# A trunk layer in split fp32: products of both token halves alternate, every second one from the last column to the first

## The reference

```
h = rms_norm(x, mix_pre_gain);  proj = h @ w_in            # 2048 x 10752
q, k, v, gm_uv, s5_u, gates = split(proj)
y_a = stick_breaking_attention(q, k, v) @ w_br_a           # 1024 x 2048
y_b = spatial_gating(gelu(gm_uv)) @ w_br_b                 #  512 x 2048
y_c = s5_layer(s5_u, ...) @ w_br_c                         #  512 x 2048
merged = g0 * y_a + g1 * y_b + g2 * y_c                    # g = sigmoid(gates)
x = x + rms_norm(merged @ w_out, mix_post_gain)
x = x + rms_norm(memory_cross_attention(rms_norm(x), rms_norm(mem), ...), xattn_post_gain)
gt, up = split(rms_norm(x, ffn_pre_gain) @ w_ffn_in)       # 2048 x 11264
x = x + rms_norm((silu(gt) * up) @ w_ffn_out, ffn_post_gain)  # 5632 x 2048
```

## Time and profile before

| | |
|---|---|
| time, median of 3 runs | 1493.7 us (1493.33 to 1494.33) |
| span of the profiled execution | 1491.6 us |
| TensorE busy | 1481.7 us (99%), 6712 matmuls |
| VectorE busy | 1137.2 us (76%) |
| ScalarE busy | 835.4 us (56%) |
| GpSimd busy | 151.4 us (10%) |
| HBM | 199 GB/s over the span |

### The profile page before, as it was taken

The page is one execution under the profiler, slowest core; times in us unless marked ns, Lnnn a source line. Parts: engine busy times, 40 slices in busy tenths (PEclk is TensorE's granted clock), DMA queues, the critical chain, the costliest instruction groups (busy, mean ns, idle before and its releaser), DMA issues.

```text
span 1491.6 us, 19212 instructions
## 1 busy us (share of the span) xinstructions
PE 1481.7 (99%) x6712; PEld 1220.6 (82%) x6712; DVE 1137.2 (76%) x1353; ACT 835.4 (56%) x1018; POOL 151.4 (10%) x286
## 2 busy tenths in 40 slices
PE   9999999999999999999999999999999999999997
PEld 7888887888888888888888888888888888888886
DVE  6878988855554577657576788888888888887897
ACT  6645455565666544656678455555555555555554
POOL 0000000140220000000000221012222221100000
PEclk9999999999999999999999999999999999999999
DMA  9755555565555655856463666766666667656564
GB/s 342 235 186 178 182 180 186 189 208 187 188 192 171 239 183 185 334 195 211 161 197 116 198 209 221 230 212 216 209 212 199 198 217 236 231 173 213 187 208 169
DMA packets 89859, 305.08 MB, mean 205 GB/s; under 512 B 13056, under 2 KB 13568, under 8 KB 88768
## 3 DMA queue, kind: packets, MB, share of 16 engines
q1 hardware_dynamic: 80144, 285.12, 57.6%
q0 software_dynamic: 9216, 18.63, 3.9%
q10 hardware_dynamic: 432, 0.45, 0.1%
HBM read 294.19 MB, written 2.10 MB: 199 GB/s over the span
## 4 chain that ended last, share of the span: by engine, by line
PE 99%; DMA 0%; DVE 0%; SPq 0%; ACT 0%; issue 0%; DVEq 0%
PE acc L1808 10%; PE acc L1809 10%; PE acc L1810 10%; PE acc L2128 5%; PE acc L2131 5%; PE acc L2130 5%; PE side L2130 5%; PE side L2131 5%; PE side L2128 5%; PE side L1808 4%; PE side L1809 4%; PE side L1810 4%; PE tr L1808 3%; PE tr L1809 3%; PE tr L1810 3%; PE side L2093 2%
## 5 line engine op out<-in xcount | busy, mean ns | idle before, releaser
L548 ACT ACTIVATE w_hi<-raw 128x1024 fp32r<-128x1024 f32 x299 | 315.1, 1060 | 295.4 <-PE acc L2131 90.2
L1001 DVE TENSOR_TENSOR w_lo<-raw,w_hi 128x1024 fp32r<-128x1024 f32 x262 | 320.9, 1227 | 202.0 <-ACT w_hi L529 197.7
L1006 DVE TENSOR_TENSOR w_lo<-raw,w_hi 128x1024 fp32r<-128x1024 f32 x315 | 381.5, 1222 | 102.8 <-ACT w_hi L548 92.9
L529 ACT ACTIVATE w_hi<-raw 128x1024 fp32r<-128x1024 f32 x262 | 276.9, 1059 | 281.3 <-PE acc L1810 165.6
L1808 PE MATMUL acc<-w_hi,xT_hi 128*128 128x512 f32 x504 | 198.3, 393 | 0.5 <-DVE w_lo L1001 0.5
L1810 PE MATMUL acc<-w_hi,xT_lo 128*128 128x512 f32 x504 | 196.3, 389 | 0.0
L1809 PE MATMUL acc<-w_lo,xT_hi 128*128 128x512 f32 x504 | 196.3, 389 | 0.0
L503 POOL DMA_DIRECT2D hT_st<-h_blk x176 | 93.6, 540 | 492.1 <-DVE h_blk L1073 453.6
L1808 PEld LDWEIGHTS acc<-w_hi,xT_hi 128*128 128x128 f32 x504 | 94.6, 188 | 22.6 <-issue 2.6
L1810 PEld LDWEIGHTS acc<-w_hi,xT_lo 128*128 128x128 f32 x504 | 94.6, 188 | 20.0
L1809 PEld LDWEIGHTS acc<-w_lo,xT_hi 128*128 128x128 f32 x504 | 94.7, 188 | 18.9
(11 more groups left out here) (468 smaller groups left out, 2747.3 us busy)
## 6 DMA issues: line engine op xcount, KB each, us to landing
raw<-in_units SPq DMA_DIRECT2D x530, 512.0 KB, 3.9
hT_st<-h_blk POOLq DMA_DIRECT2D x176, 32.0 KB, 1.8
x_tok<-in_x SPq DMA_DIRECT2D x4, 512.0 KB, 5.9
qkT<-qk_blk POOLq DMA_DIRECT2D x64, 32.0 KB, 2.9
xres<-in_x POOLq DMA_DIRECT2D x1, 2048.0 KB, 11.0
m_raw<-in_mem_t POOLq DMA_DIRECT2D x1, 2048.0 KB, 8.6
mq<-in_mem POOLq DMA_DIRECT2D x1, 2048.0 KB, 15.4
x_raw<-in_x_t SPq DMA_DIRECT2D x6, 256.0 KB, 6.4
```

The source lines that it names most:

```text
L529: a_.activation(w_hi[:, j % RING], raw[:, j % RING], ACT.Copy).then_inc(hi_ready, 1)
L548: a_.activation(w_hi[:, v % RING], raw[:, slots[block]], ACT.Copy).then_inc(hi_ready, 1)
L1001: v_.tensor_tensor(w_lo[:, s], raw[:, s], w_hi[:, s].bitcast(F32), ALU.subtract).then_inc(lo_ready, 1)
L1006: v_.tensor_tensor(lo[:, v % RING], raw[:, slot], hi[:, v % RING].bitcast(F32), ALU.subtract).then_inc(lo_ready, 1)
```

## The change

Both loops hand a k tile to a new helper, `turnabout`. It runs the six products of one k tile for both halves in the order (half 0, w_lo), (half 1, w_lo), (half 1, w_hi), (half 0, w_hi), (half 0's low part, w_hi), (half 1's low part, w_hi). The second, fourth and sixth are given their moving tile and their output through `back`, which turns the columns round: the product reads columns 511 to 0 and writes columns 511 to 0. The numbers that arrive in the bank are the same products. The waits for `acc_taken` of both halves now stand ahead of the chunk's first product, and half 0's last product is the last but one of the chunk.

In `chunk`:

```diff
-                    for h in range(HALVES):
-                        if first and j == 0 and lag:
+                    if first and j == 0 and lag:
+                        for h in range(HALVES):
                             pe.wait_ge(acc_taken[h], g + (1 - lag))
-                        tok = slice(h * P, (h + 1) * P)
-                        for k in range(UK):
-                            kt = k0 + UK * j + k
-                            begin, end = first and j == 0 and k == 0, last and j == units - 1 and k == UK - 1
-                            pe.matmul(bank(b, h), hi[:, kt, tok], w_hi[:, s, k], start=begin, stop=False)
-                            pe.matmul(bank(b, h), hi[:, kt, tok], w_lo[:, s, k], start=False, stop=False)
-                            mm = pe.matmul(bank(b, h), lo[:, kt, tok], w_hi[:, s, k], start=False, stop=end)
-                        if h == 0 and last and j == units - 1:
-                            mm.then_inc(acc0_full, 1)
-                    mm.then_inc(unit_used, 1)
+                    for k in range(UK):
+                        kt = k0 + UK * j + k
+                        begin, end = first and j == 0 and k == 0, last and j == units - 1 and k == UK - 1
+                        done = turnabout([bank(b, 0), bank(b, 1)], lambda h: hi[:, kt, h * P:(h + 1) * P],
+                                         lambda h: lo[:, kt, h * P:(h + 1) * P], w_hi[:, s, k], w_lo[:, s, k], (begin, begin), end)
+                        if last and j == units - 1 and k == UK - 1:
+                            done[0].then_inc(acc0_full, 1)
+                    done[1].then_inc(unit_used, 1)
```

More of the change, by code:

```diff
@@ L2124, in plain_units @@
                             pe.wait_ge(acc_taken[h], begins[h])
[L2125 to L2135, removed]
+                    for k in range(UK):
+                        kt, top = kt0 + UK * j + k, j == 0 and k == 0
+                        done = turnabout([bank(b, 0), bank(b, 1)], lambda h: hi[:, kt, h * P:(h + 1) * P],
+                                         lambda h: lo[:, kt, h * P:(h + 1) * P], whi[:, k], wlo[:, k],
+                                         [top and begins[h] is not None for h in range(HALVES)], last and j == count - 1 and k == 1)
+                        if last and b == 1 and j == count - 1 and k == 1:
+                            done[0].then_inc(acc0_full, 1)
+                    done[1].then_inc(unit_used, 1)
             for i in range(1, 11):
```

## The result

The changed kernel takes 1542.91 us (1542.71 to 1543.54, 4 runs) beside 1494.01 us of the kernel before (1493.33 to 1494.55, 4 runs): ratio 1.0328, 95% interval 1.0313 to 1.0342. I had forecast 1503.2 us with a range up to 1530. The direction was right and the loss is five times what I summed.

A forecast was written before the change was run, and what follows sets the result against it. TensorE, busy 99% of the span, was taken as the bound. Border stalls of 7.7 + 1.1 + 0.7 = 9.5 us with free reversal gave 1503.2 us (+0.64%); range for 8 in 10: 1,438 to 1,530 us.

The forecast's parts named there:

- The borders: Chunk borders in the projection stage and behind `U_MV`: waiting for both banks' evictions costs 7.7 + 1.1 + 0.7 = 9.5 us.
- part 1: The 2,676 reversed products: taken to cost 0, from a row with jumping reads; upper bound +607 us.
- small price: Rival: each reversed product costs 1 to 10 ns more, +3 to +27 us, 1,506 to 1,530 us; chance 0.08.
- Half rate: Rival: columns go half as fast backwards, 0.227 us more per reversed product, +607 us, about 2,110 us; chance 0.10.
- the turn wait: Rival: a product re-entering the bank just written waits for its drain, 0.16 us each, +290 us, about 1,793 us; chance 0.05.
- The saved gap: Rival: turning saves the 13.3 ns between products, up to 71 us, 1,432 us, or 1,468 on half the products; chance 0.18.
- Hidden after all: Rival: the drain at chunk borders is hidden, time within 3 us of before; semaphores exclude it at eight borders.
- a price backwards: Sign: a step of 0.23 to 0.45 us on the reversed products alone would show that reversal costs time.
- on the reversed products alone: Condition of a sign: only reversed products' steps would lengthen, to 0.23 to 0.45 us, if reversal costs time.
- the FFN, where I had forecast nothing: Sign: the FFN's span grows by nothing and gains no new waits, while the projection stage grows by 9 us.

The follow-up runs named there:

- new_fwd: The changed kernel with its new order of products but every product forward, none reversed: 1505.4 us, ratio 1.0076.
- mov_only: The changed kernel with only the moving tiles turned and the outputs written forward: 1542.7 us (one run).
- blocks_swap: The kernel before, with the loops' moving tiles read as two blocks of 256 columns, second block first, each forward: 1494.6 us (one run).
- old_alt: The kernel before, in its old order of products, with the second, fourth and sixth product of each half reversed: 1510.3 us, ratio 1.0110.
- out_only: The changed kernel with only the outputs turned and the moving tiles read forward: 1505.4 us (one run).
- line_turn: The kernel before, with the loops' moving tiles read in rising groups of 4 columns, each group from last column to first: 1493.8 us (one run).
- turn_blocks: The changed kernel with turned products reading and writing two blocks of 256 columns, each from its last column to its first: 1521.2 us (one run).

## Why the prediction was wrong

**The borders: right, in mechanism, place and size.** From the last product of the unit ahead of a border to the last product of the unit behind it, less one unit's time (2720 or 2813.3 ns), and less what the kernel before has at the same border, in us:

| border | predicted | new_fwd | changed kernel |
|---|---|---|---|
| into the projection loop | 1.45 | 1.47 | 1.45 |
| first to second chunk, each of four | 1.56 | 1.61 | 1.56 |
| between passes, each of three | 0.36 | 0.34 | 0.29 |
| behind `U_MV` | 0.7 | 0.70 | 0.64 |
| sum | 9.5 | 9.6 | 9.2 |

Each border came out within 0.1 us. The restart in it was split otherwise than I had it: in `new_fwd` the evictions end at 119.57 + 1.27 = 120.84 and the first product stands at 120.98, 0.14 us later instead of 0.05, and the products behind it lose 0.12 us instead of 0.15 (0.07 of it in the first step, 120.98 to 121.28). `new_fwd` costs 11.3 us in all. In its trace the stretch from the first to the last unit is 11.7 us longer; the 2.0 us beyond the borders lie in the FFN's output part, where TensorE waited in four places for a late `w_lo`. The rows ahead of them show ScalarE waiting for VectorE's sums of weights (L1014), and once, at 1457.39, for 2.29 us for weights from HBM. The traces of the new order show none (`mov_only`) to four such places. Of those of the old order five show none, the kernel before among them, and three show one or two, up to 0.6 us together (`blocks_swap`). So such a place is not the new order's alone; whether the order makes them more frequent or one execution differs from another was not tested and stays open.

**The step that failed: part 1, "I take 0, since the row is the nearest that exists".** The row had rising runs of 32 columns with jumps. It gives durations, which I had myself called latency; but in the trace of the kernel before the steps on both lines are alike too, 0.215 to 0.216 us. So it is true of what it shows: jumps are free, as `blocks_swap` confirms at full width (2720 ns). It says nothing about falling addresses, and I let it decide for them. A falling read costs 6.67 ns: 2,676 x 6.67 = 17.8 us.

**The second failure: an interaction that no rival held.** Re-entry costs 8 x 6.67 ns x 446 = 23.8 us, more than the reversal. I priced a turn, but put it in the bank that had just been written, where it is free (`old_alt`, `out_only`), and at 160 ns. That a product now starts where the last one stopped I had written down only as a possible gain.

**The sum as it was.** 17.8 + 23.8 = 41.6 us for the steps, 9.2 for the borders and 0.3 for one late `w_lo` in the FFN (at 1390.7) make 51.1; measured from the first to the last unit are 49.3. Most of the 1.8 us between them is in stages with side products between the units: the 64 gate units grew by 5.2 us instead of 6.0, since a unit that follows side products grew by 33 to 58 ns there and not by 93. My price would have had to be 15.6 ns a reversed product; the "small price" rival ended at 10, and its chance was 0.08.

**The rivals.** Half rate (+607 us) and the turn wait (+290 us) didn't happen. On the writing side the Trainium skill ("Advanced Engine Details and Errata", section PSUM Cachelines) could be read against a falling output; by the reading in pairs it costs nothing, and `out_only` agrees with that one: 0 ns. On the reading side the Trainium skill ("Advanced Engine Details and Errata", section SBUF Cachelines) says that accesses which stay in one 16-byte line run at full speed; `line_turn` agrees with 0 ns. The 6.67 ns of groups in falling order are what the runs show. The saved gap went the other way: a product that starts its read where the last read of the tile stopped pays for it. "Hidden after all" was excluded as argued.

**The signs I had named.** The step grew, which I had read as "a price backwards"; but "on the reversed products alone" failed as a test, since the changed kernel's growth is spread over forward and reversed steps alike (0.227 to 0.240) in two patterns. Only sums over a whole unit could be compared. And the FFN, where I had forecast nothing, grew by 17 us.

## What to carry to other kernels

Products of this size can write their output reversed for nothing, but keep the moving tile rising: a falling read costs 6.67 of 227 ns here, and starting at the columns of the tile where the last read ended costs the same again. When two banks that were completed one after the other are made to complete together, write down who asks for them next and price two evictions plus the restart at each such border; it comes out to a tenth of a microsecond. And where the trace has no row for an access pattern, the nearest row bounds it only in the property that it shares: a small price on each of thousands of products on the only busy engine deserves more chance than the round zero.

## What the runs showed of the hardware

- A product of 128 x 512 fp32r reads its moving tile in 226.7 ns with rising 16-byte groups and 233.3 ns with falling ones; order inside a group (`line_turn`), a swap of halves (`blocks_swap`), and the direction of the output (`out_only`) make no difference.
- A read that begins with the columns with which the previous read of the same tile ended costs a further 6.67 ns (2813 beside 2760 ns a unit in `turn_blocks`); reading the same tile twice in the same direction costs nothing (`new_fwd`, 2720 ns).
- The unit times of products of 512 columns are multiples of 6.67 ns apart (2720, 2760, 2787, 2800, 2813). What in the engine has that grain stays open, and so does why a unit with reversed products of 256 columns (2,800 ns) was faster than one with forward ones (2,843).
